# Key norms moved amid the values' blocks of a projection, and the RWKV body's instruction order changed on three engines

## What is computed

```
u  = h @ w_in                                 # projection
z  = w[0]*u[t-1] + w[1]*u[t] + w[2]*u[t+1]    # token shift
kk = heads(k * k_k)
kk = kk / max(sqrt(sum(kk*kk over a head)), 1e-12)
# per head and direction, for every token:
sa = S @ kk_t
S  = S * w_t - sa (kk_t * a_t)^T + v_t kd_t^T
y  = S @ r_t
```

## Time and profile before

| | |
|---|---|
| median of 3 runs | 5098.99 us (5093.28 to 5112.98) |
| the profiled execution | 5105.09 us, span of its instructions 5103.3 us |
| granted TensorE clock, mean | 0.97 |
| busy, share of the span | PE 92%, PEld 55%, DVE 50%, ACT 36%, POOL 27% |
| projection, body of pairs | from about 2371 to 3031 us |
| recurrence | from 3031 to about 4822 us |

### The profile page before, as it was taken

The page is one execution under the profiler, slowest core; times in us unless marked ns, Lnnn a source line. Parts: engine busy times, 40 slices in busy tenths (PEclk is TensorE's granted clock), DMA queues, the critical chain, the costliest instruction groups (busy, mean ns, idle before and its releaser), DMA issues. The chain is left out here.

```text
span 5103.3 us, 123816 instructions
## 1 busy us (share of the span) xinstructions
PE 4705.9 (92%) x50814; PEld 2817.4 (55%) x50814; DVE 2535.0 (50%) x4204; ACT 1836.3 (36%) x4413; POOL 1383.1 (27%) x2884
## 2 busy tenths in 40 slices
PE   6999997999999998999999969899999989989699
PEld 3666663333333334454444437777787777778544
DVE  2444444665666661232343355555555555555376
ACT  1212111444444431132222225455555555555332
POOL 1111111333332320000000005444454444445343
PEclk8999997999999998999999989999999999999899
DMA  5222223000000005432322246666666666666575
GB/s 210 95 83 93 85 75 120 5 23 24 24 24 24 23 6 220 146 135 63 124 74 69 66 129 172 166 169 173 171 183 171 158 178 171 181 165 167 154 229 174
DMA packets 958460, 602.74 MB, mean 118 GB/s; under 512 B 661382, under 2 KB 903686, under 8 KB 943881
## 3 DMA queue, kind: packets, MB, share of 16 engines
q1 hardware_dynamic: 871434, 572.86, 38.3%
q10 hardware_dynamic: 86528, 22.82, 2.1%
HBM read 398.63 MB, written 196.88 MB: 117 GB/s over the span
## 5 line engine op out<-in xcount | busy, mean ns | idle before, releaser
L934 PE MATMUL at_bS<-at_qT,at_kT 97*64 97x512 f32 (+1 forms) x2368 | 604.9, 596 | 15.1 <-ACT at_pT L1032 14.5
L1639 PE MATMUL p_bU<-keep_hT,p_slab 128*128 128x512 f32 (+1 forms) x1504 | 588.6, 554 | 8.0 <-DMA p_slab<-in_o_w_in_dram 7.4
L1069 DVE TENSOR_REDUCE at_mx<-at_bM 128x1 f32<-128x512 f32 (+1 forms) x656 | 394.0, 627 | 352.2 <-PE at_bM L899 351.2
L2216 PE MATMUL rw_bank<-keep_rw_hg,rw_slab 128*128 128x256 f32 x2048 | 481.5, 389 | 8.9 <-DMA keep_rw_hg<-scratch_hT 6.9
L1032 ACT ACTIVATE at_pT<-at_bS 128x512 f32<-128x512 f32 (+1 forms) x592 | 342.4, 591 | 396.8 <-PE at_bS L934 377.3
L1639 PEld LDWEIGHTS p_bU<-keep_hT,p_slab 128*128 128x128 f32 x1504 | 286.6, 191 | 305.7 <-issue 288.4
L2216 PEld LDWEIGHTS rw_bank<-keep_rw_hg,rw_slab 128*128 128x128 f32 x2048 | 382.5, 192 | 69.3 <-DMA keep_rw_hg<-scratch_hT 7.7
L2519 DVE TENSOR_TENSOR rw_S<-rw_bank,rw_dec 128x128 f32<-128x128 f32 x288 | 83.0, 288 | 649.3 <-PE rw_bank L2196 644.0
L2021 POOL TENSOR_TENSOR rw_g_at<-rw_g_at,rw_g_prod 64x14 f32<-64x14 f32 (+6 forms) x1008 | 328.6, 326 | 79.0
L856 POOL TENSOR_TENSOR at_sum_pool<-at_sum_pool,at_pT 128x512 f32<-128x512 f32 x192 | 244.0, 1271 | 372.2 <-ACT at_pT L1032 354.8
L2019 POOL TENSOR_TENSOR rw_g_prod<-rw_g_at 64x14 f32<-64x14 f32 (+6 forms) x1008 | 321.3, 319 | 79.1
(11 more groups left out here) (289 smaller groups left out, 9926.4 us busy)
## 6 DMA issues: line engine op xcount, KB each, us to landing
keep_wide<-scratch_heads SPq DMA_DIRECT2D x144, 512.0 KB
keep_rw_hg<-scratch_hT SPq DMA_DIRECT2D x64, 1024.0 KB
rw_XB<-scratch_inverses SPq DMA_DIRECT2D x576, 64.0 KB
keep_wide<-scratch_lora SPq DMA_DIRECT2D x144, 128.0 KB
scratch_bv<-rw_bv SPq DMA_DIRECT2D x144, 128.0 KB
scratch_products<-rw_NB SPq DMA_DIRECT2D x288, 64.0 KB, 4.0
scratch_y<-rw_ysb ACTq DMA_DIRECT2D x288, 64.0 KB, 4.4
scratch_heads<-p_z SPq DMA_DIRECT2D x17, 1024.0 KB, 4.9
```

Source lines behind the costliest of these rows:

```text
L934: last = pe.matmul(bS[rows, g % 3, 0:nq * P], kT[:, s, k * P + VH * x:k * P + VH * x + VH], qT[:, s, q0 * P:(q0 + nq) * P], start=True, st ...
L1069: nc.vector.tensor_reduce(mx[:, j, piece:piece + 1], bM[:, (FIRST_ITEM[b] + i) % 2, 0:n], AX.X, ALU.max).then_inc(max_red, 1)
L1639: last = pe.matmul(bU[:, n % 4, 0:w], slab[:, i, k, :], hT[:, k, tok:tok + w], start=(k == 0), stop=(k == KD - 1))
L2216: last = pe.matmul(DENSE[:, GT * j:GT * (j + 1)], slab[:, j, q, :], hg[:, x.slot, q, :], start=(q == 0 and j == 0), stop=(q == KD - 1), sk ...
```

## The change

In the projection the products with `same` move from behind the tenth block to between the values' blocks: four after the second (`NORMS_AFTER = 1`), the fifth after the third. ScalarE's roots, VectorE's chain to `kk` and SP's stores of `kk` move with them: VectorE now makes `kk` ahead of the values' taps, and SP stores `kk` ahead of the values' rows and of the second slab's load.

In the recurrence, on TensorE: `step_sa` of chunk 0 goes ahead of turning V; the scores of the first piece go all ahead of `step_begin` of chunk 1, two chunks of them beside `step_values`; turning B goes behind `step_begin` of chunk 1; `first_order` goes beside `step_values` of chunk 3, and half of the last scores beside `step_begin` of chunk 3. On ScalarE: `take_r1` of chunk 0 goes up by three of K's copies and by `take_dense`, all four copies of V stand behind `take_sa`, and `take_dense` behind them. On VectorE `queries` goes from behind `weights` to behind `add_orders` in the next body.

```diff
...
         PB = 2 * NB
+        NORMS_AFTER = 1
         c_l, s_l = sem("p1_consts_loaded"), [sem(f"p1_slab{i}_loaded") for i in range(3)]
...
                             load(i, at)
-                    sp.wait_ge(kk_done, p + 1)
-                    store(heads[:, 1, :], kk, kk_st)
-                    sp.dma_start(heads[:, 2, 0:CTX], kk[:, 0:CTX]).then_inc(kk_st, 16)
+                        if i == 0:
+                            sp.wait_ge(kk_done, p + 1)
+                            store(heads[:, 1, :], kk, kk_st)
+                            sp.dma_start(heads[:, 2, 0:CTX], kk[:, 0:CTX]).then_inc(kk_st, 16)
...
             def _(pe):
-                def blocks(i, base, n0, first):
-                    for b in range(first, NB):
+                def norms(p, parts):
+                    for x in parts:
+                        c, w = SBLK[x]
+                        pe.wait_ge(root, NS * p + max(0, x - 3))
+                        pe.matmul(bS[:, x % 4, 0:w], same[:], kq[:, c:c + w], start=True, stop=True).then_inc(ss_mm, 1)
+                def blocks(i, base, n0, first, end=NB):
+                    for b in range(first, end):
                         tok, _, w = BLK[b]
...
                     base = PRE + PB * p
-                    for i in range(2):
-                        pe.wait_ge(s_l[i], 16 * p + 32)
-                        blocks(i, base, NB * i, 0)
-                    pe.wait_ge(c_l, 16 * 5)
-                    pe.wait_ge(kq_done, p + 1)
-                    for x, (c, w) in enumerate(SBLK):
-                        pe.wait_ge(root, NS * p + max(0, x - 3))
-                        pe.matmul(bS[:, x % 4, 0:w], same[:], kq[:, c:c + w], start=True, stop=True).then_inc(ss_mm, 1)
+                    pe.wait_ge(s_l[0], 16 * p + 32)
+                    blocks(0, base, 0, 0)
+                    pe.wait_ge(s_l[1], 16 * p + 32)
+                    for b in range(NB):
+                        blocks(1, base, NB + b, b, b + 1)
+                        if b == NORMS_AFTER:
+                            pe.wait_ge(c_l, 16 * 5)
+                            pe.wait_ge(kq_done, p + 1)
+                            norms(p, range(0, 4))
+                        if b == NORMS_AFTER + 1:
+                            norms(p, range(4, NS))
...
                     nc.scalar.activation(z[:, zs, lo:TZ], u[:, us, 1 + lo:TZ + 1], ACT.Identity, scale=shift[:, 1, tile]).then_inc(z1, 1)
+                def roots(p, parts):
+                    for x in parts:
+                        c, w = SBLK[x]
+                        a.wait_ge(ss_mm, NS * p + x + 1)
+                        nc.scalar.activation(rn[:, c:c + w], bS[:, x % 4, 0:w], ACT.Sqrt).then_inc(root, 1)
...
                             evict(NB * i + b, base, b, slot)
+                            if i == 1 and b == NORMS_AFTER:
+                                a.wait_ge(kk_done, p)
+                                roots(p, range(0, 4))
+                            if i == 1 and b == NORMS_AFTER + 1:
+                                roots(p, range(4, NS))
                         if i == 0:
...
                             nc.scalar.activation(kq[:], z[:, 1, :], ACT.Square, scale=k_k[:, bass.ds(p, 1)]).then_inc(kq_done, 1)
-                    a.wait_ge(kk_done, p)
-                    for x, (c, w) in enumerate(SBLK):
-                        a.wait_ge(ss_mm, NS * p + x + 1)
-                        nc.scalar.activation(rn[:, c:c + w], bS[:, x % 4, 0:w], ACT.Sqrt).then_inc(root, 1)
...
                     links = 3 + 4 * p
-                    for i in range(2):
-                        shift_taps(1 - i, 1 - i, bass.ds(p + (0, KD)[i], 1), 3 + 2 * p + i, links + i)
+                    shift_taps(1, 1, bass.ds(p, 1), 3 + 2 * p, links)
                     v.wait_ge(root, NS * (p + 1))
                     nc.vector.tensor_scalar(rn[:], rn[:], 1e-12, None, ALU.max).then_inc(dchain, 1)
+                    v.wait_ge(dchain, links + 2)
+                    nc.vector.reciprocal(rn[:], rn[:]).then_inc(dchain, 1)
                     v.wait_ge(dchain, links + 3)
-                    nc.vector.reciprocal(rn[:], rn[:]).then_inc(dchain, 1)
-                    v.wait_ge(dchain, links + 4)
                     v.wait_ge(kk_st, 48 * p)
...
                                                    op0=ALU.mult, op1=ALU.mult).then_inc(kk_done, 1)
+                    shift_taps(0, 0, bass.ds(p + KD, 1), 4 + 2 * p, links + 3)
...
                         bonus(k)
-                        turn(k, 2)
                     if has[0]:
                         step_sa(n, 0)
+                    if has[3]:
+                        turn(k, 2)
                     if has[4]:
...
                     if has[3]:
+                        scores_free(k, 0, 0)
+                    if has[0]:
+                        step_values(n, 1, (lambda i: scores(k, 0, 0, (i,))) if has[3] else None)
+                    elif has[3]:
+                        scores(k, 0, 0, (0, 1))
+                    if has[3]:
+                        scores(k, 0, 0, (2, 3))
+                    if has[0]:
+                        step_begin(n, 1)
+                    if has[3]:
                         turn(k, 1)
-                    if has[0]:
-                        step_values(n, 1)
-                    if has[3]:
-                        scores_free(k, 0, 0)
-                        scores(k, 0, 0, (0, 1))
-                    if has[0]:
-                        step_begin(n, 1, (lambda i: scores(k, 0, 0, (2 + i,))) if has[3] else None)
-                    elif has[3]:
-                        scores(k, 0, 0, (2, 3))
                     if has[0]:
...
                         step_end(n, 2)
-                    if has[1]:
+                    if has[0]:
+                        step_values(n, 3, (lambda i: first_order(m, i)) if has[1] else None)
+                    if has[3]:
+                        scores_free(k, 1, 1)
+                        scores(k, 1, 1, (0, 1))
+                    if has[0]:
+                        step_begin(n, 3, (lambda i: scores(k, 1, 1, (2 + i,))) if has[3] else None)
+                    elif has[3]:
+                        scores(k, 1, 1, (2, 3))
+                    if has[1] and not has[0]:
                         for d in range(2):
                             first_order(m, d)
-                    if has[3]:
-                        scores_free(k, 1, 1)
-                        scores(k, 1, 1, (0, 1, 2, 3))
-                    if has[0]:
-                        step_values(n, 3)
-                        step_begin(n, 3)
                     if has[3]:
...
                         a.wait_ge(set_up, 3)
-                    take_dense(n.on(-1))
                     if has[0]:
                         take_r1(n, 0)
-                        if n.since(1):
-                            store_y(n.on(-1), 0)
-                    if has[3]:
+                    if has[2]:
+                        turned(n.on(2), 0, 0, 1)
                         for e in range(2):
-                            turned(k, 2, 0, e)
+                            turned(n.on(2), 0, 1, e)
+                    if has[0] and n.since(1):
+                        store_y(n.on(-1), 0)
                     if has[0]:
...
                     if has[3]:
-                        for e in range(2):
-                            turned(k, 2, 1, e)
+                        for h in range(2):
+                            for e in range(2):
+                                turned(k, 2, h, e)
+                    take_dense(n.on(-1))
+                    if has[3]:
                         decay_of_chunks(k)
...
                     if has[3]:
-                        for h in range(2):
-                            for e in range(2):
-                                turned(k, 0, h, e)
+                        turned(k, 0, 0, 0)
...
                             add_orders(n, d, 1)
+                    if has[3]:
+                        queries(k)
                     if has[3]:
...
                         weights(l)
-                        queries(l)
```

## The result

The changed kernel takes 5132.53 us, median of 6 runs (5124.51 to 5136.61); beside it the kernel before took 5101.47 (6 runs, 5093.28 to 5112.98). The ratio is 1.0054, 95% interval [1.0044, 1.0064]: slower by half a per cent. Forecast were 5118 and a range of 5090 to 5142.

The account below looks back on a forecast made before the run. TensorE was taken as nearly full but paced by ScalarE's copy of Y at the restarts of chunk 1 and the last chunk. Head +43, chunk 3 +2 and -11, projection -15: +19 on 5099, so 5118 us, range 5090 to 5142.

Parts of the forecast that it names:

- The deciding point: At chunk 1's restart TensorE would wait about 1.3 us for ScalarE's copy of Y instead of for XT.
- Rival A: In the recurrence the wait for XT is simply won, saving 42.2 us besides the projection's 15: 5042 us; chance 0.10.
- The head, 0.73 us a body: Body up to chunk 1's step_sa: copy of Y 0.19 later, restart to step_sa 0.54 longer; 59 bodies, +43 us.
- Chunk 3, +0.04: Behind the last chunk's restart, 0.63 us becomes 0.67 with scores beside; over 59 bodies +2 us.
- Absorption: Ahead of chunk 3's restart, shorter work gains 0.6 us in 19 passes stopped by "issue": -11 us.
- rival B: In the recurrence's lulls all 25.5 us of "issue" idle go instead of 11: sum +5, 5104 us; chance 0.15.
- my own forecast: Whole kernel at 5118 us, own range 5108 to 5128; chance 0.45.
- D: The projection gives nothing, as squares come later or VectorE's chain holds the next pair: +34, 5133 us; chance 0.05.
- C: In the recurrence nothing is absorbed and all 67 bodies pay: +36, 5135 us; chance 0.25.
- The turning's mode: Two more tiling-mode changes a body drain TensorE: one inside the 0.54, one ahead of the wait for Y; sum unchanged.
- The projection, -15: Norms' wait falls 0.6 us a pair, 4.2 for seven; the hand-over to the recurrence gains 11.5: -15 us.

Follow-up runs that it names:

- e4: The changed kernel with ScalarE's copies of Y and R1 of chunk 1 ahead of the dense copy and the two first rates: 5090.12 us, ratio 0.9969.
- e12: The kernel before with one part of the change alone, VectorE adding the last order ahead of the queries: 5088.39 us, ratio 0.9962 to the kernel before.
- e3: The changed kernel with the turning of B issued ahead of step_begin of chunk 1: 5102.39 us, ratio 0.9993 to the kernel before.
- e5: The changed kernel with all four groups of the last scores issued ahead of chunk 3's restart again: 5115.49 us, ratio 1.0017 to the kernel before.
- e1: The projection as changed with the recurrence of the kernel before: 5097.04 us, ratio 0.9981 to the kernel before.
- e6: The changed kernel with B turned before chunk 1's restart, ScalarE's Y and R1 copies earlier there, all scores before chunk 3's restart: 5082.74 us, ratio 0.9955.
- e9: e6 with V turned ahead of chunk 0's step_sa on TensorE again, as in the kernel before: 5077.67 us, ratio 0.9939 to the kernel before.

## Why the prediction was right, point by point

**The deciding point** held: "the wait for XT turns into a wait for Y". The wait at chunk 1 is 1.19 where about 1.3 was forecast, the restart follows the copy by 0.05 in both chunks (in the last one the copy ends at 4061.75 and TensorE restarts at 4061.80), and e4, which only moves ScalarE's copies, takes the loss away and more. Rival A fell with the changed kernel itself, whose bodies got longer without the wait for XT. Nor is that wait simply won with TensorE's order kept: in e12 12 of 42 us come through in the recurrence, though there V's copies hold TensorE, and not Y's, as I had reasoned.

**The head, 0.73 us a body.** Measured 0.85 (from the end of one body to step_end of chunk 1, 11.91 to 12.76, medians of the dense bodies). The part behind the restart, 0.54, came out exactly (0.67 to 1.21). The copy of Y is 0.33 later and not 0.19: step_sa starts 2.55 behind chunk 0's copy (4043.88 to 4046.43), and I had left it at the 2.45 of V's old place. From step_sa to the copy it is 4.06, forecast 4.02.

**Chunk 3, +0.04.** This is the step that failed: +0.43. I took the restart with scores beside it from chunk 1, 0.67. But there step_sa follows, a group of the same 64x64 form, and it began among the scores of the kernel before (L2098), which still start 0.18 behind it, so that they cost only 0.15 (without them e3 has 0.52 there):

```profile
4041.92 0.28 PE L2098 MATMUL rw_bank<-rw_AR,rw_Bc 64*64 64x128 f32 x2
```

In the last chunk a turning follows, and it begins only as the last scores end. With 59 bodies this is 25 us raw, and e5 gives 17 us back.

**Absorption.** I let 11 us of "issue" idle vanish; it was 22 (68.1 to 45.9), nearer to rival B's 25. The wait for sa lost 9 more (4.6 us now); in the kernel before it was:

```profile
PE rw_bank L2196 <- ACT rw_sa L2351: 13.5, 11, 1.8
```

Of 59 x 1.28 = 75.5 raw, 39.5 arrived in the recurrence. So the sum was 23 us too low in chunk 3 and 7 in the head, and about 25 too little was absorbed: the errors mostly cancelled, and 5118 was nearer than its working deserved. The measured 5132.5 lies in the range, but outside the 5108 to 5128 that I gave my own forecast, and next to D's 5133 and C's 5135. D fell with e1, in which the projection gives about 10 us; C fell with the 36 us that did not arrive.

In e3, e4 and e5 too the common body says more than the time: 43, 64 and 24 us of raw sum, 30, 42 and 17 in the time. Why is not shown. That slower bodies swallow "issue" idle does not fit all runs: from 3090 to 4780 us it is 57.9 us in e3 and 51.4 in e4, but 46.3 in e5, and 47.4 in e6, whose bodies are as short as those of the kernel before. e9, which is e6 with V turned earlier, has 66.2, so the order on TensorE counts for more here than the body's length. The Trainium skill (Runtime: NRT & Kernel Launch, Instruction fetch mechanics) calls crossing a block of code mostly hidden. Whether these stalls are late code no run here shows.

**The turning's mode.** Four transposes between groups of 64x64 take 0.58 to 0.59 us of TensorE's time, wherever they stand (4046.81 to 4047.40, 4051.44 to 4052.02, and K's in the earlier trace rows). In the kernel before, V was turned behind the bonus product, itself 128*128, and took 0.44 of TensorE's time, against 0.59 (what a group adds to TensorE's busy time behind the group ahead, over the ordinary bodies of each trace; the busy times of bodies above are from the same bodies where no window is shown). I wrote that the other changes of form "lie ahead of the wait for Y, so the sum stays". That held for the changed kernel, where e4 does the same work in 42 us less, but this rest, 0.35 us a body more of TensorE's own work, is what kept e6's bodies long, as far as e9's shorter ones show it. The Trainium skill (TensorEngine Tiling (Array Packing), Key Properties) says that a changed tiling mode drains TensorE: the trace agrees, and the price here is about 0.15 us at V, and 0.36 a body in all by e9, which has two changes less than e6 for the same matmuls.

**The projection, -15.** Measured -12.6 in the profile and about -10 in e1. The wait for the squares is 0.86 (forecast 1.0) and the gap 17.24 (forecast 20 to 22). Not in the sum: the wait for p_u, 0.67 in each pair. I looked at what the norms wait for and not at what they cover. The first block of a pair waits until the last block of the pair before is copied out (L1645, `pe.wait_ge(ev, base + max(0, n - 3))` with n = 0). In the changed kernel that copy (the second row) starts right behind the block, and ScalarE's shift and table load follow it:

```profile
2926.80 0.59 ACT L1673 COPY p_u<-p_bU 128x512 f32<-128x512 f32 x1 [6.43 <-PE p_bU L1647]
2933.66 0.58 ACT L1673 COPY p_u<-p_bU 128x512 f32<-128x512 f32 x1 [6.28 <-PE p_bU L1647]
2934.46 2.23 ACT L1679 ACTIVATE p_z<-p_u,keep_rw_shift 128x2306 f32<-128x2306 f32 x1 [0.21 <-ACT p_u L1673]
2936.70 1.28 ACT L1673 ACT_TABLE_LOAD   x1
```

Before the change TensorE had the norms to do meanwhile, 5.9 us with their wait (2997.02 to 3002.89 in the earlier trace rows). Now it comes straight to the next pair and goes on at 2934.30, 0.06 behind the end of the copy:

```profile
2919.73 13.90 PE L1647 MATMUL p_bU<-keep_hT,p_slab 128*128 128x512 f32 x32
2934.30 26.04 PE L1647 MATMUL p_bU<-keep_hT,p_slab 128*128 128x256 f32 x68 [0.68 <-ACT p_u L1673]
```

The norms' old place had a use: 0.86 and 0.67 now stand for the 1.58 of before, so the pairs won next to nothing, and the gain is at the hand-over. The wait comes from how the program counts. The first block writes bank 0 of `bU`, which the ninth block of the pair before had used, and whose copy (the first row) was over by 2927.4. A count that lets it go then might win the 5.4 us; that was not run.

## What to carry to other kernels

Where an engine restarts a constant few hundredths of a microsecond behind another engine's instruction, that is the point to cost an order from: work ahead of it is free, work behind it counts, and the cheapest repair was here to move the releasing instruction itself (e4: 42 us for two copies of 0.27 us). A wait in the list is worth only its distance to the next constraint, here Y's copy and V's copies within half a microsecond of XT, so expect a fraction. Two edits can win the same slack (e3's and e4's, at chunk 1). And when the waits are nearly gone, the bound is the engine's own work in the new order, which can be longer than in the old one for the same instructions (e9 against e6).

## What the runs showed of the hardware

- The same matmuls of a body (544 and 543 in the records) kept TensorE busy 22.86 us in one order and 23.21 in the other, at a granted clock of 1.00 in both.
- ScalarE's ACT_TABLE_LOAD takes 1.28 us, and the profile has two of them in each pair in either place of the roots (ahead of the roots, and between the shift and the next copy), so moving the roots saved none and cost none.
- A group of 64x64 form started among scores of the same form (4041.74), and one of 128*128 form started 0.33 behind the start of the last four of them (4062.53 to 4062.86, in the changed kernel's last chunk), 0.06 ahead of their end. The term that failed hung on this.
